# A one-core transformer block kernel whose layer changes are taken in token halves

## The chip, the core and the metric

The kernel runs on one core of one Trainium2 chip. The metric is the device time of one launch in microseconds, the median of the runs shown.

## What is computed

Five residual layers of 1024 channels over 512 tokens, all in float32: a gated delta-rule mixer, a short-convolution mixer, a mixer of block attention, pooling and spatial gating, a cross attention over 256 memory rows, and a gated feed-forward part. Around each mixer `f` stand two norms:

```python
h = rms_norm(x, pre_norm_w[i])
y = f(h)                          # products with w_in, the mixer, a product with w_out
x = x + rms_norm(y, post_norm_w[i])
```

`rms_norm` multiplies a token's row by one over the root of its mean square, then by a weight for each channel. It works on each token by itself, so one half of the tokens can be normed before the other.

## The kernel before, in words

Activations lie channel-major: a tile is 128 channels by 512 tokens, and `xT`, `h_hi`, `h_lo` and `y_T` hold eight tiles each (index `k`). Every large product is made of three (`product3`, L739): each operand is split into a rounded part `hi` and the remainder `lo`, and hi by hi, hi by lo and lo by hi are added in PSUM. One chunk is 128 output channels by 512 tokens: 8 tiles by 3 products, 24 matmuls, in one of the banks.

**Weights** come in slabs of 1024 by 256, two chunks each, in the order of `plan` (L286). SyncE loads a slab into one of two ring slots. ScalarE makes `w_hi` (`split_hi`, L1533) once the slab two before it has been used by TensorE; VectorE makes `w_lo` (`split_lo`, L2160). Seventeen slabs have their `w_lo` from GpSimd (L2899, L2906), among them `SC0`, `MIX0` and `FF1`, the first slabs of the layers 1, 2 and 4. TensorE waits for `split_ready` of a slab (`next_slab`, L705). All four queues run in the order written.

**A seam** is the passage from a layer's output product to the next layer's first chunks. The change touches three: the first (layer 0 to 1), the second (1 to 2) and the third (3 to 4). At each, before:

- TensorE makes the eight output chunks. In the first and second seam they stand in banks 0 to 7 (`out_tile` L831, `wide_out` L855), with 16 input tiles in two passes; in the third they rotate over four banks (`pair3`).
- ScalarE's `post_norm` (L1562) squares each chunk into `sq` and copies it into `y_T`. VectorE's `sum_squares` (L2191) adds the squares in `rs`. TensorE sums over the channels with a matmul by ones (`out_sum`, L770), in plain float32, and ScalarE's `inverse_rms` (L1550) makes the root's inverse by Ln and Exp.
- VectorE's `post_norm` (L2206) then takes tile by tile: multiply by `rs` (L2217), add to `xT` (L2221), and after ScalarE's `h_hi` (`pre_norm`, L1606) the remainder `h_lo` (L2225). A tree of seven additions (L2239) follows, for the next norm.
- TensorE's `first_four` (L784) first issues 14, 8 and 14 products that nobody reads (`keep_clock`, L779), in the seams one, two and three. Then it follows the tiles: for tile `k` four products with `h_hi` and two with `h_lo` for two chunks of the first slab, and half a tile's work (three products) of the second slab's two chunks. Nine such halves, 27 products, are left when the first slab is done, and `norm_sum` (L765) stands among them.
- The second slab is split by halves: ScalarE takes one half of its `w_hi` (`split_hi_half`, L1544), VectorE the other (`split_lo_halves`, L2168).

At the second seam, 32 transposes for a bias (L1228) and the ScalarE copies of them (L1905) also lie in this passage.

## Time and profile before

| What | us |
|---|---|
| Median of 3 runs (1804.18 to 1804.68) | 1804.19 |
| The profiled execution's own time | 1804.97 |
| Its span, first to last instruction | 1803.2 |
| TensorE busy in it (10559 matmuls) | 1777.8 |
| VectorE, ScalarE, GpSimd busy | 991.3, 722.9, 140.9 |

The profile shows one execution. Busy TensorE time contains overlapping matmuls, since a matmul's duration includes its way through the array; its rate is read from the distance between starts.

### The profile page before, as it was taken

The page shows a single profiled execution, that of the slowest core. Times are in us where ns is not written, and L with a number is a line of the kernel's source. Part 1 is how long each engine was busy: PE and PEld are TensorE (multiplying, and loading weights), DVE is VectorE, ACT ScalarE, POOL GpSimd, SP SyncE. Part 2 cuts the span into 40 slices and gives each one's busy share as a digit, 9 for nine tenths or more (in the row PEclk, how much of TensorE's full clock was granted, in tenths as well). Part 3 has the DMA queues.
Part 4 walks back from the last instruction along what each step waited for, and adds up shares of the span by engine and source line. Part 5 has one row for each costly group of instructions (what it writes and reads, how often), then busy time and mean ns, then how long its engine had stood idle before and what let it go on. Part 6 is the DMA issues. An engine that isn't in the chain of part 4 may idle for free.

```text
span 1803.2 us, 26545 instructions
## 1 busy us (share of the span) xinstructions
PE 1777.8 (99%) x10559; PEld 1437.7 (80%) x10559; DVE 991.3 (55%) x1666; ACT 722.9 (40%) x1382; POOL 140.9 (8%) x108
## 2 busy tenths in 40 slices
PE   8999999999999999999999999999999999999999
PEld 6788888887887888888888788468887778888887
DVE  4645656466636544454443746744424587777434
ACT  5645656547435212211124533754223532222324
POOL 1113031130002000000000101520000100000000
PEclk9999999999999999999999999999999999999999
DMA  6422212122235332222333451013313222223221
GB/s 194 84 54 76 63 49 78 55 71 62 83 109 124 110 100 93 93 93 93 101 106 98 91 117 48 24 48 117 117 47 117 70 93 93 93 94 110 98 77 65
DMA packets 183184, 158.18 MB, mean 88 GB/s; under 512 B 36978, under 2 KB 179887, under 8 KB 183051
## 3 DMA queue, kind: packets, MB, share of 16 engines
q1 hardware_dynamic: 172672, 152.88, 27.8%
q0 software_dynamic: 1248, 3.19, 1.2%
q10 hardware_dynamic: 9163, 0.72, 0.4%
q8 instruction: 70, 1.15, 0.3%
q14 instruction: 31, 0.25, 0.0%
HBM read 152.77 MB, written 3.73 MB: 87 GB/s over the span
## 4 chain that ended last, share of the span: by engine, by line
PE 90%; DVE 4%; ACT 3%; issue 1%; DMA 1%; ACTq 0%; SPq 0%; POOL 0%; DVEq 0%
PE bank L744 13%; PE bank L746 13%; PE bank L745 13%; PE bank L845 5%; PE bank L847 5%; PE bank L846 5%; PE bank L945 4%; PE bank L947 4%; PE bank L946 4%; PE bank L734 4%; PE bank L1072 1%; PE bank L1083 1%; PE bank L1139 1%; PE bank L1094 1%; PE bank L1338 1%
## 5 line engine op out<-in xcount | busy, mean ns | idle before, releaser
L1542 ACT ACTIVATE w_hi<-ring 128x2048 fp32r<-128x2048 f32 x122 | 234.0, 1918 | 535.6 <-PE bank L746 376.1
L744 PE MATMUL bank<-h_hi,w_hi 128*128 128x512 f32 x1024 | 400.4, 391 | 2.2 <-DVE w_lo L2165 2.0
L746 PE MATMUL bank<-h_hi,w_lo 128*128 128x512 f32 x1024 | 398.5, 389 | 0.0
L745 PE MATMUL bank<-h_lo,w_hi 128*128 128x512 f32 x1024 | 398.4, 389 | 0.0
L2165 DVE TENSOR_TENSOR w_lo<-ring,w_hi 128x2048 fp32r<-128x2048 f32 x105 | 240.4, 2290 | 247.9 <-ACT w_hi L1542 247.9
L744 PEld LDWEIGHTS bank<-h_hi,w_hi 128*128 128x128 f32 x1024 | 192.2, 188 | 44.9 <-issue 3.6
L745 PEld LDWEIGHTS bank<-h_lo,w_hi 128*128 128x128 f32 x1024 | 192.2, 188 | 40.2 <-issue 0.5
L746 PEld LDWEIGHTS bank<-h_hi,w_lo 128*128 128x128 f32 x1024 | 192.2, 188 | 40.1
L845 PE MATMUL bank<-h_hi,w_hi 128*128 128x512 f32 x432 | 170.5, 395 | 1.7 <-DVE arena L2854 1.0
L847 PE MATMUL bank<-h_hi,w_lo 128*128 128x512 f32 x432 | 168.3, 390 | 0.0
L846 PE MATMUL bank<-h_lo,w_hi 128*128 128x512 f32 x432 | 168.2, 389 | 0.0
L2903 POOL TENSOR_TENSOR w_lo<-ring,w_hi 128x2048 fp32r<-128x2048 f32 x16 | 73.5, 4591 | 1059.3 <-ACT w_hi L1542 1059.3
L945 PE MATMUL bank<-h_hi,w_hi 128*128 128x512 f32 x368 | 151.2, 411 | 0.0
L947 PE MATMUL bank<-h_hi,w_lo 128*128 128x512 f32 x368 | 143.9, 391 | 0.0
L946 PE MATMUL bank<-h_lo,w_hi 128*128 128x512 f32 x368 | 143.6, 390 | 0.0
L2260 DVE SCALAR_TENSOR_TENSOR arena<-arena,cols 128x511 f32<-128x511 f32 x120 | 90.1, 751 | 14.8 <-DVE arena L2260 0.3
L845 PEld LDWEIGHTS bank<-h_hi,w_hi 128*128 128x128 f32 x432 | 81.1, 188 | 18.6 <-issue 1.5
L847 PEld LDWEIGHTS bank<-h_hi,w_lo 128*128 128x128 f32 x432 | 81.1, 188 | 17.1
L846 PEld LDWEIGHTS bank<-h_lo,w_hi 128*128 128x128 f32 x432 | 81.2, 188 | 15.9
L947 PEld LDWEIGHTS bank<-h_hi,w_lo 128*128 128x128 f32 x368 | 69.1, 188 | 15.3
L945 PEld LDWEIGHTS bank<-h_hi,w_hi 128*128 128x128 f32 x368 | 69.2, 188 | 14.9 <-issue 1.9
L946 PEld LDWEIGHTS bank<-h_lo,w_hi 128*128 128x128 f32 x368 | 69.4, 188 | 11.8
(449 smaller groups left out, 2508.7 us busy)
## 6 DMA issues: line engine op xcount, KB each, us to landing
ring<-in_sc_w_in SPq DMA_DIRECT2D x32, 1024.0 KB, 5.4
ring<-in_gdn_w_in SPq DMA_DIRECT2D x24, 1024.0 KB, 5.4
ring<-in_w_up SPq DMA_DIRECT2D x22, 1024.0 KB, 5.1
ring<-in_gdn_w_out SPq DMA_DIRECT2D x8, 1024.0 KB, 5.2
ring<-in_sc_w_out SPq DMA_DIRECT2D x8, 1024.0 KB, 5.2
ring<-in_w_down SPq DMA_DIRECT2D x8, 1024.0 KB, 5.2
ring<-in_w_in SPq DMA_DIRECT2D x4, 1024.0 KB, 5.7
ring<-in_w_mk SPq DMA_DIRECT2D x4, 1024.0 KB, 5.2
```

Of the source, the lines that this page charges most:

```text
L744: pe.matmul(o, a_hi(k), b_hi(k), start=(k == tiles[0]), stop=False)
L745: pe.matmul(o, a_hi(k), b_lo(k), start=False, stop=False)
L746: mm = pe.matmul(o, a_lo(k), b_hi(k), start=False, stop=(k == tiles[-1]))
L845: pe.matmul(o, w_hi[:, st["slab"], w], h_hi[:, k, :], start=(a == 0 and k == 0), stop=False)
L846: pe.matmul(o, w_hi[:, st["slab"], w], h_lo[:, k, :], start=False, stop=False)
L847: mm = pe.matmul(o, w_lo[:, st["slab"], w], h_hi[:, k, :], start=False, stop=(a == last and k == kt - 1))
L945: pe.matmul(psum[b][:, :], w_hi[:, st["slot"], w], h_hi[:, k, :], start=(k == 0), stop=False)
L946: pe.matmul(psum[b][:, :], w_hi[:, st["slot"], w], h_lo[:, k, :], start=False, stop=False)
L947: mm = pe.matmul(psum[b][:, :], w_lo[:, st["slot"], w], h_hi[:, k, :], start=False, stop=(k == KD - 1))
L1542: act.activation(w_hi[:, plan[n]["pair"], :], ring[:, n % 2, :], ACT.Copy).then_inc(w_hi_ready, 1)
L2165: dve.tensor_tensor(w_lo[:, plan[n]["pair"], :], ring[:, n % 2, :], w_hi[:, plan[n]["pair"], :].bitcast(F32), ALU.subtract)\
L2260: ins = dve.scalar_tensor_tensor(out=dst[:, s:S], in0=src[:, 0:S - s], scalar=weight(taps - 1 - s), in1=dst[:, s:S], op0=ALU.mult, op1=ALU ...
```

## The change

The last two output chunks of the three layers share one bank for each half of the tokens: columns 0 to 255 are the even chunk and 256 to 511 the odd one. TensorE computes the whole first half of the tokens (`halves_done`, n = 0), then the second. Square, copy, sum and root of the first half are issued while the second is computed. The next layer's tiles 0 to 4 come as ten units of 256 tokens (five of the first half, five of the second), tiles 5 to 7 whole. TensorE follows these 13 units (`first_units`): the second slab's products for the units 0 to 3 are made together at unit 4, and from then on each unit has six products of either slab. `keep_clock` is no longer called at the seams. The half splits are gone: the second slab's `w_hi` is made whole by ScalarE between the units 2 and 3, its `w_lo` whole by VectorE before unit 5. The `w_lo` of `SC0`, `MIX0` and `FF1` goes from GpSimd to VectorE. `norm_sum` moves: into chunk 4 at the first seam, among the bias transposes at the second, to the end of `first_units` at the third. The bias transposes go behind `first_units`. At the first seam chunks 4 to 6 use banks 4 to 6.

```diff
+        HALVED, BY_HALF = (0, 1, 3), 5
+        units_of = lambda layer: [(k, half) for half in halves for k in range(BY_HALF)] + [(k, every) for k in range(BY_HALF, KD)] \
+            if layer in HALVED else [(k, every) for k in range(KD)]
...
-            def first_four(parts, idle):
...
-                keep_clock(4, idle)
...
+            def half_out(slab, bank, k, n, opens=False, closes=False):
+                for side in range(2):
+                    o, w = bank[:, halves[side]], slice(k * 256 + P * side, k * 256 + P * side + P)
+                    pe.matmul(o, w_hi[:, slab, w], h_hi[:, k, halves[n]], start=(opens and k == side == 0), stop=False)
+                    pe.matmul(o, w_hi[:, slab, w], h_lo[:, k, halves[n]], start=False, stop=False)
+                    mm = pe.matmul(o, w_lo[:, slab, w], h_hi[:, k, halves[n]], start=False, stop=(closes and k == KD - 1 and side == 1))
+                return mm
+            def halves_begun():
...
+                for k in range(KD):
+                    for n in range(2):
+                        mm = half_out(slab, psum[6 + n], k, n, opens=True)
...
+            def halves_done(slab, banks, totals, opens=False, within=lambda k: None):
...
+                for n in range(2):
+                    for k in range(KD):
...
+                        if k == KD - 3:
+                            pe.wait_ge(square_used, base + KD - 2)
+                            pe.matmul(totals[n][:, 0:S // 2], ones, rs[:, halves[n]], start=True, stop=False)
+                        if n and k == 0:
+                            half_sum(totals, 0)
+            def half_sum(totals, n):
+                pe.wait_ge(square_ready, 8 * st["layer"] + KD - 1 + n)
+                pe.matmul(totals[n][:, 0:S // 2], ones, sq[:, 0, halves[n]], start=False, stop=False)
+                pe.matmul(totals[n][:, 0:S // 2], ones, sq[:, 1, halves[n]], start=False, stop=True).then_inc(square_used, 1)
+            def first_units(totals):
...
+                for u, (k, i) in enumerate(units):
+                    pe.wait_ge(h_hi_ready, at + u + 1)
+                    high_products(slab, banks, k, i)
+                    if u == BY_HALF - 1:
+                        slab1 = next_slab()
+                        banks += [take_bank(None) for _ in range(2)]
+                        for earlier in units[:u]:
+                            second_products(slab1, banks, *earlier)
+                    pe.wait_ge(h_ready, at + u + 1)
+                    low_products(slab, banks, k, i)
+                    if u == BY_HALF - 2:
+                        half_sum(totals, 1)
+                        st["layer"] += 1
+                    if u >= BY_HALF - 1:
+                        second_products(slab1, banks, k, i)
```

ScalarE, `post_norm` and `pre_norm`:

```diff
+                    if early is not None and k == KD - 2:
...
+                        half_squares(st["open"][0][0], layer, 0)
+                        half_copies(st["open"][0][0], layer, 0)
+                        st["layer"] += 1
+                        half_rms(totals[0], layer, 0)
+                        return
...
+                for u, (k, i) in enumerate(units_of(layer - 1)):
+                    act.wait_ge(x_ready, units_before(layer - 1) + u + 1)
+                    act.activation(h_hi[:, k, i], xT[:, k, i], ACT.Copy, scale=PRE[layer](k)).then_inc(h_hi_ready, 1)
+                    if i.stop == S:
+                        act.activation(y_T[:, k, :], xT[:, k, :], ACT.Square).then_inc(x_squared, 1)
+                        between(k)
+                    elif u == BY_HALF - 3:
+                        banks, totals, second = st["open"]
+                        split_hi(second)
+                    elif u == BY_HALF - 2:
+                        half_squares(banks[1], layer - 1, 1)
+                    elif u == BY_HALF - 1:
+                        half_copies(banks[1], layer - 1, 1)
+                        half_rms(totals[1], layer - 1, 1)
```

VectorE, `post_norm`:

```diff
+                dve.wait_ge(rms_ready, roots_before(layer) + 1)
+                for u, (k, i) in enumerate(units):
+                    opens_half = i.start and k == 0
+                    if opens_half:
+                        split_lo(second)
+                        low_part(u - 1)
+                        dve.wait_ge(rms_ready, roots_before(layer) + 2)
+                    scaled(k, i)
+                    if u and not opens_half:
+                        low_part(u - 1)
+                    added(k, i)
```

GpSimd:

```diff
-            split_lo(SC0)
...
-            split_lo(MIX0)
...
-            split_lo(FF1)
```

## Rows read from the trace of the kernel before

**Rows 1.** The page: busy time (part 1), chain by engine (part 4).
```profile
PE 1777.8 (99%) x10559; PEld 1437.7 (80%) x10559; DVE 991.3 (55%) x1666; ACT 722.9 (40%) x1382; POOL 140.9 (8%) x108
...
PE 90%; DVE 4%; ACT 3%; issue 1%; DMA 1%; ACTq 0%; SPq 0%; POOL 0%; DVEq 0%
```

**Rows 2.** Timeline of PE (start, duration, us): full-width products, three issues apart.
```profile
557.71 0.39 PE L845 MATMUL bank<-h_hi,w_hi 128*128 128x512 f32 x1
...
558.39 0.39 PE L845 MATMUL bank<-h_hi,w_hi 128*128 128x512 f32 x1
```

**Rows 3.** Timeline of PE: products over 256 columns, 33 issues apart.
```profile
1034.86 0.28 PE L744 MATMUL bank<-w_hi,h_hi 128*128 128x256 f32 x1
...
1038.82 0.28 PE L744 MATMUL bank<-w_hi,h_hi 128*128 128x256 f32 x1
```

**Rows 4.** Timeline, first seam: from the last product to the next layer's.
```profile
559.75 1.02 PE L774 MATMUL bank<-rs,masks 128*128 128x512 f32 x2
559.95 0.60 ACT L1560 ACTIVATE sq<-bank 128x512 f32<-128x512 f32 x1 [3.31 <-PE bank L847]
...
560.61 1.12 PE L776 MATMUL bank<-sq,masks 128*128 128x512 f32 x2
...
561.77 0.69 ACT L1552 ACTIVATE rs<-bank,small 128x512 f32<-128x512 f32 x1 [0.64 <-PE bank L776]
...
563.16 0.69 DVE L2217 TENSOR_TENSOR arena<-arena,rs 128x512 f32<-128x512 f32 x1 [0.68 <-ACT rs L1554]
...
564.61 0.72 ACT L1610 ACTIVATE h_hi<-xT,cols 128x512 fp32r<-128x512 f32 x1 [1.49 <-DVE xT L2221]
...
565.37 0.75 DVE L2225 SCALAR_TENSOR_TENSOR h_lo<-xT,cols,h_hi 128x512 fp32r<-128x512 f32 x1 [0.19 <-ACT h_hi L1610]
...
565.48 0.47 PE L820 MATMUL bank<-h_hi,w_hi 128*128 128x512 f32 x1 [0.56 <-ACT h_hi L1610]
```

**Rows 5.** Timeline at the first seam: the end of the first four chunks.
```profile
581.08 4.54 DVE L2239 TENSOR_TENSOR arena<-arena 128x512 f32<-128x512 f32 x7
...
582.83 1.92 ACT L1542 ACTIVATE w_hi<-ring 128x2048 fp32r<-128x2048 f32 x1 [1.94 <-PE bank L827]
...
585.54 2.28 DVE L2165 TENSOR_TENSOR w_lo<-ring,w_hi 128x2048 fp32r<-128x2048 f32 x1
...
585.97 1.02 PE L768 MATMUL bank<-arena,masks 128*128 128x512 f32 x2
...
587.06 0.39 PE L811 MATMUL bank<-h_lo,w_hi 128*128 128x512 f32 x1
...
589.98 0.47 PE L744 MATMUL bank<-h_hi,w_hi 128*128 128x512 f32 x1 [0.23 <-DVE arena L2540]
```

**Rows 6.** Timeline of PE, second seam: sum, transposes, first row chunk.
```profile
1003.51 1.02 PE L774 MATMUL bank<-rs,masks 128*128 128x512 f32 x2
...
1005.42 1.22 PE L1231 MATMUL bank<-masks,arena 31*128 31x31 f32 x32
...
1034.06 0.36 PE L744 MATMUL bank<-w_hi,h_hi 128*128 128x256 f32 x1
```

**Rows 7.** Timeline of PE, third seam: sum, fifth chunk's first product.
```profile
1420.94 1.02 PE L774 MATMUL bank<-rs,masks 128*128 128x512 f32 x2
...
1450.79 0.39 PE L744 MATMUL bank<-h_hi,w_hi 128*128 128x512 f32 x1
```

**Rows 8.** Groups by line and shape (busy us, mean ns): 256 columns.
```profile
L1984 ACT ACTIVATE arena<-bank,small 128x256 f32<-128x256 f32 x4 | 1.9, 471 | 9.5 <-PE bank L746 9.5
L2292 DVE TENSOR_TENSOR ws<-arena,ws 128x256 fp32r<-128x256 f32 x1 | 0.4, 421 | 0.0
```

**Rows 9.** The page, part 5: the slab remainders that POOL computes.
```profile
L2903 POOL TENSOR_TENSOR w_lo<-ring,w_hi 128x2048 fp32r<-128x2048 f32 x16 | 73.5, 4591 | 1059.3 <-ACT w_hi L1542 1059.3
```

**Rows 10.** First products, and their stretch (PE, PEld, DVE, ACT, POOL, PEclk, DMA, GB/s).
```profile
17.74 0.47 PE L890 MATMUL bank<-h_hi,w_hi 128*128 128x512 f32 x1 [2.66 <-DVE h_lo L2288]
...
16.00:24.00 8.00, 6.26 (x20) 4.84 (x21) 6.67 (x9) 6.89 (x11) 4.57 (x1) 0.79 0.64 169
```

More of the change, by code:

```diff
@@ L494, in build @@
         square_sum = y_T[:, 0, :]
+        HALVED, BY_HALF = (0, 1, 3), 5
+        halves, every = [slice(0, S // 2), slice(S // 2, S)], slice(0, S)
+        roots_before = lambda layer: 2 * layer + sum(n < layer for n in HALVED)
+        units_of = lambda layer: [(k, half) for half in halves for k in range(BY_HALF)] + [(k, every) for k in range(BY_HALF, KD)] \
+            if layer in HALVED else [(k, every) for k in range(KD)]
+        units_before = lambda layer: sum(len(units_of(n)) for n in range(layer))
         rs_squared = sq[:, 0, :]
@@ L800, in first_four @@
-                    low_products(slab, first, k)
-                for n in range(KD - 1, 2 * KD):
-                    half_tile(slab1, later, n)
-                    if n == KD + 3:
-                        norm_sum()
-            def half_tile(slab, banks, n):
-                k, side = n // 2, n % 2
-                b, w = banks[side], slice(k * 256 + P * side, k * 256 + P * side + P)
-                pe.matmul(psum[b][:, :], w_hi[:, slab, w], h_hi[:, k, :], start=(k == 0), stop=False)
-                pe.matmul(psum[b][:, :], w_hi[:, slab, w], h_lo[:, k, :], start=False, stop=False)
-                mm = pe.matmul(psum[b][:, :], w_lo[:, slab, w], h_hi[:, k, :], start=False, stop=(k == KD - 1))
-                if k == KD - 1:
-                    mm.then_inc(chunk_done, 1)
@@ new lines, in second_products @@
+            def second_products(slab, banks, k, i):
+                for side in range(2):
+                    o, w = psum[banks[2 + side]][:, i], slice(k * 256 + P * side, k * 256 + P * side + P)
+                    pe.matmul(o, w_hi[:, slab, w], h_hi[:, k, i], start=(k == 0 and i.start == 0), stop=False)
+                    pe.matmul(o, w_hi[:, slab, w], h_lo[:, k, i], start=False, stop=False)
+                    mm = pe.matmul(o, w_lo[:, slab, w], h_hi[:, k, i], start=False, stop=(k == KD - 1))
+                    if k == KD - 1:
+                        mm.then_inc(chunk_done, 1)
@@ L819, in high_products @@
+            def high_products(slab, banks, k, i):
+                for side, b in enumerate(banks[0:2]):
                     w = slice(k * 256 + P * side, k * 256 + P * side + P)
-                    pe.matmul(psum[b][:, :], w_hi[:, slab, w], h_hi[:, k, :], start=(k == 0), stop=False)
-                    pe.matmul(psum[b][:, :], w_lo[:, slab, w], h_hi[:, k, :], start=False, stop=False)
-            def low_products(slab, banks, k):
-                for side, b in enumerate(banks):
+                    pe.matmul(psum[b][:, i], w_hi[:, slab, w], h_hi[:, k, i], start=(k == 0 and i.start == 0), stop=False)
+                    pe.matmul(psum[b][:, i], w_lo[:, slab, w], h_hi[:, k, i], start=False, stop=False)
@@ L826, in low_products @@
+            def low_products(slab, banks, k, i):
+                for side, b in enumerate(banks[0:2]):
                     w = slice(k * 256 + P * side, k * 256 + P * side + P)
-                    mm = pe.matmul(psum[b][:, :], w_hi[:, slab, w], h_lo[:, k, :], start=False, stop=(k == KD - 1))
+                    mm = pe.matmul(psum[b][:, i], w_hi[:, slab, w], h_lo[:, k, i], start=False, stop=(k == KD - 1))
                     if k == KD - 1:
@@ L1569, in post_norm @@
                         split_hi(early)
-                    if k == KD - 1 and early is not None:
-                        split_hi_half(early + 1)
+                    if early is not None and k == KD - 2:
+                        first, totals = st["chunk"], (psum[4:6] if wide else [psum[7], psum[6]])
+                        st["open"] = [psum[6 + n if wide else (first + n) % 4][:, :] for n in range(2)], totals, early + 1
+                        half_squares(st["open"][0][0], layer, 0)
[3 more added lines that the diff above has]
+                        return
                     act.wait_ge(chunk_done, n + 1)
@@ L2208, in post_norm @@
                 layer = st["layer"]
[L2209 removed]
+                sum_squares(ahead, beside, KD - 1 if second is None else KD - 2)
                 if second is not None:
[L2211 to L2212 removed]
+                    split_lo(second - 1)
                 if layer == 0:
                     dve.wait_ge(x_back, KD)
[L2216 to L2217 removed]
@@ new lines, in post_norm @@
+                dve.wait_ge(rms_ready, roots_before(layer) + 1)
[9 more added lines that the diff above has]
+                    added(k, i)
+                    if i == every and k:
+                        between(k)
```

186 lines of the change are left out of this document (94 added, 92 removed).

## The prediction

> **What bounds the kernel.** The page comes first: TensorE is busy for 1777.8 us of a span of 1803.2, and 90% of the chain that ended last lies on it [rows 1]. A change can gain only where TensorE waits or issues work that nobody reads, and it loses with every nanosecond that a needed product takes longer. The waits of TensorE name the seams, so the timelines of the three seams are what decides. At the first, the last product's successor starts at 559.75 and the next layer's first product at 565.48: 5.7 us, filled by the sum of squares, fourteen idle products and a wait [rows 4]. I count a seam from the end of its last output product to the start of the fifth chunk (the first row chunk at the second seam): 589.98 - 559.75 = 30.2 us, 1034.06 - 1003.51 = 30.6, 1450.79 - 1420.94 = 29.9 [rows 4 to 7]. Needed in each are 96 products and the norm's sum. Three products take 0.68 us, so one takes 0.2267 [rows 2], and 96 take 21.8. The norm's sum takes 587.06 - 585.97 less a product, 0.86 [rows 5]. What is left, **7.6, 7.9 and 7.2 us**, is all that the change can work on. That is 22.7 us in all.
>
> **What the halves cost.** Thirty-three issues of a product over 256 columns take 3.96 us, 0.120 each [rows 3]. Two halves take 0.240 against 0.2267 for one whole: 13.3 ns more for each product that is split. The first and second seam split 48 in the first pass of the output product, 48 in its last slab, and 5 tiles x 4 chunks x 3 = 60 in the next layer: 156, 2.1 us. The third has no first pass: 108, 1.4 us. In all 420, 5.6 us. The rows have other operands in the two roles, but TensorE's work for them is the same in kind, and I take their value. The ends are no loss at all (width alone) and twice it. The Trainium skill, "TensorE: Matmul & The Clock Gate", section "Back-to-back issue gap", gives an issue's gap as its columns at 2.4 GHz and 2.5 ns more; by it 420 splits would cost 1.1 us, and my sum would come out 4.5 us lower. The rows speak against it here.
>
> The sums of squares go from two float32 matmuls of full width to six of half width. At 0.43 us for a half (0.86 halved) that is 2.6 us a seam, all of it between needed products; before, its 1.7 us lay in the 5.7. If a half took as long as a whole, it would be 2.6 us more a seam; width counts in rows 2 and 3, so I stay near the half.
>
> **The chain of the first half.** Let 0 be the end of the first half's products. ScalarE starts its squares 0.20 after it and the sum can start at 0.86, as in rows 4. TensorE is then 0.72 us (six halves) into the second half: a wait of 0.1. The Ln comes at 2.02 (561.77 - 559.75). From it to the multiplication take 1.39 us and on to `h_hi` 1.45 [rows 4]. At half width ScalarE saves about 0.21 an operation (0.69 to 0.47) and VectorE 0.27 (0.69 to 0.42) [rows 4, 8], so `h_hi` starts at 2.02 + 0.97 + 0.91 = 3.9. Then a unit takes a round of `h_hi` 0.51, remainder 0.48, addition 0.42: 1.4 us. The third `h_hi` ends at 3.9 + 2.8 + 0.5 = 7.2. TensorE's second half takes 48 x 0.12 + 0.1 + 0.86 + 0.43 = 7.2 too. So units 0 to 2 are ready just in time and the old hole of 5.7 us is gone. This is the gain.
>
> **The wait in the middle.** ScalarE's `split_hi` of the second slab stands behind unit 2 in its queue and waits for the end of the second half (its pair of `w_hi` is in use till then): 7.4 to 9.3, since a slab takes 1.92 [rows 5]. Behind it wait `h_hi` of unit 3 (to 9.8) and the second half's squares (to 10.3). VectorE's remainder of unit 3 and the addition of unit 4 end at 10.6, then its `split_lo` of 2.28 [rows 5] ends at 12.9. TensorE has from 7.2 on 24 + 4 halves and the second sum, 3.4 + 0.86 = 4.2 us, and needs that slab next. It waits 12.9 - 7.2 - 4.2 = 1.5 us, in one or two pieces. Ends: 0 and 3. The second half's own chain is no wait: `rs` is ready about 12.9, unit 5 at 14.6, while TensorE has 24 + 2 + 6 halves (3.8 us) up to 16.8. From there a unit is 12 halves, 1.44 us, against VectorE's 1.4, and a whole tile 2.7 against some 2.15. TensorE is the bound again and VectorE gets ahead. Its tree of 4.54 us [rows 5] is done in time.
>
> **The wait at the end.** This is what speaks against the change. The third slab's `w_hi` may be written when the first slab is done. Before, 27 products and the norm's sum (7.0 us) were left at that point. Now six are left, 1.36 us, since the second slab keeps step. The third slab needs ScalarE 0.26 after it, then 1.92, VectorE 2.28, and about 0.1 for signals: 4.55 us [rows 5]. TensorE **waits 3.2 us** at the first seam. At the other two the next chunk needs also a bank that VectorE empties only behind that `split_lo` (0.69 us, as rows 4 have it): 5.25 - 1.36 - 0.86 (the norm's sum, which runs meanwhile) = 3.0. At the second seam the 32 bias transposes (1.1 us in the issues of rows 6, where they lay in the old hole) and the turning of `rs` fit into these 3.0, and cost nothing more. The bank wait that before stood ahead of the fifth chunk goes by the new banks 4 to 6, and is in the 7.6.
>
> **The rest.** GpSimd's three `w_lo` of 4.59 us [rows 9] become VectorE's of 2.28: VectorE has nothing else between the sixth square and the root, so nothing waits. SyncE's load of the fourth slab waits for the second slab's split and comes some 5 us later; it is needed 15 us after. At the second seam SyncE's small loads and a conv slab are behind it and move by some 4 us; they cost nothing while the slab that follows is not issued before the third slab is split. ScalarE copies the bias after the norm's root, ahead of the row chunks, and has caught up before its third eviction.
>
> **The sum.** New, other than the 96 products and the norm's sum: first seam 2.1 + 2.6 + 0.1 + 1.5 + 3.2 = 9.5 against 7.6, so +1.9; second 2.1 + 2.6 + 0.1 + 1.5 + 3.0 = 9.3 against 7.9, +1.4; third 1.4 + 2.6 + 0.1 + 1.5 + 3.0 = 8.6 against 7.2, +1.4. Together **+4.7 us**. The profiled execution took 1804.97, 0.8 above the median of 1804.19, and would take 1809.7; the median goes to **1808.9**.
>
> **The rivals.**
> - *The halves are cheap*: a split product costs nothing beyond its columns. Then 5.6 us fall away: 1803.3. Rows 3 speak against it. 0.10.
> - *No wait in the middle*: ScalarE and VectorE get the second slab done within TensorE's 4.2 us. 4.5 us less: 1804.4. 0.18.
> - *The end is covered* (faster): the third slab is split in time, and the waits of 3.2, 3.0 and 3.0 us are not there: 1799.7. It decides at 4.55 us of TensorE work behind the first slab's last product; I count 1.36. 0.06.
> - *The clock falls*: in this trace TensorE waited 2.66 us ahead of 17.74, after small transposes, and in 16 to 24 us the granted clock was 0.79 of 2.4 GHz: 42% of 8 us at 1.2 GHz, which loses 1.7 us [rows 10]. The new waits of 3 us could do the same, now that the idle products are gone: 3 x 1.7 = 5.1, 1814.0. Against it: dense products stand ahead of each. 0.14.
> - *It doesn't do what it says*: the first half's chain is longer than the second half's products (7.2 us), and the old hole comes back in part. A unit that takes 0.35 us longer makes 1.0 a seam: 1811.9. 0.10.
>
> My forecast has the remaining 0.42; its own range is 1806.5 to 1811.5. The range reaches to the rivals on both sides but the fastest: 1803.2 to 1814.2. A difference under 0.2%, 3.6 us, can't be told from none. Slower by more (above 1807.8): 0.36 of the forecast and the last two rivals, 0.60. Same: the rest of it and the first two, 0.34. Faster: 0.06.
>
> **What would show it.** Right: no wait of TensorE at a seam's first unit; a wait for `w_lo` of the second slab of about 1 us; three waits near 3 us behind the first four chunks, released by VectorE; TensorE's issues over 256 columns at 0.12; granted clock at 2.4 GHz throughout. Wrong: the third slab's split ready before TensorE asks, a seam of under 29 us by the same count, or a clock that falls after the waits.

## The result, and the profile of the changed kernel

The changed kernel took 1812.28 us in the median of five runs (1811.08 to 1813.93), the kernel before, in the same rounds, 1804.18 (1801.99 to 1804.68): a ratio of 1.0046, 95% interval 1.0034 to 1.0057. That is 0.46% slower, 8.1 us. It lies in the range on record (1803.2 to 1814.2) and on the side that the chances favoured, but outside the likeliest case's own range, which ended at 1811.5. The profiled execution took 1813.93 with a span of 1812.1, 8.9 us more than before.

The page, busy time and chain, against [rows 1]:

```profile
PE 1782.8 (98%) x10967; PEld 1463.7 (81%) x10967; DVE 991.6 (55%) x1705; ACT 729.4 (40%) x1409; POOL 126.6 (7%) x105
...
PE 89%; DVE 4%; ACT 3%; issue 2%; DMA 1%; ACTq 0%; SPq 0%; POOL 0%; DVEq 0%
```

TensorE is busy 5.0 us longer, although the 36 idle products (8.2 us at 0.2267 each) are gone from its work, and the span is 8.9 us longer, so 3.9 us more of it are waiting. The list of TensorE's waits names the new ones (us in total, times, longest):

```profile
PE bank L750 <- DVE w_lo L2253: 4.0, 3, 3.1
PE bank L750 <- DVE arena L2939: 2.8, 1, 2.8
...
PE bank L859 <- DVE w_lo L2253: 2.1, 3, 0.7
```

L750 is the first product of an ordinary chunk, L859 the first of the second slab. The six waits for `h_hi` that the kernel before had at its seams (3.0 us) are gone; three of 0.3 us, one a seam, have come in their place. The timeline of PE at the first seam puts them in order (start, duration; in brackets the wait and its releaser):

```profile
562.26 0.28 PE L796 MATMUL bank<-h_hi,w_lo 128*128 128x256 f32 x1
562.38 0.28 PE L869 MATMUL bank<-h_hi,w_hi 128*128 128x256 f32 x1
...
587.15 0.39 PE L861 MATMUL bank<-h_hi,w_lo 128*128 128x512 f32 x1
590.64 0.50 PE L750 MATMUL bank<-h_hi,w_hi 128*128 128x512 f32 x1 [3.10 <-DVE w_lo L2253]
590.98 0.40 PE L751 MATMUL bank<-h_lo,w_hi 128*128 128x512 f32 x1
591.22 0.57 PE L752 MATMUL bank<-h_hi,w_lo 128*128 128x512 f32 x1
591.58 1.91 PE L774 MATMUL bank<-arena,masks 128*128 128x512 f32 x2
592.50 1.42 PE L750 MATMUL bank<-h_hi,w_hi 128*128 128x512 f32 x1
593.72 0.63 PE L751 MATMUL bank<-h_lo,w_hi 128*128 128x512 f32 x1
594.14 0.63 PE L752 MATMUL bank<-h_hi,w_lo 128*128 128x512 f32 x1
594.57 0.45 PE L750 MATMUL bank<-h_hi,w_hi 128*128 128x512 f32 x1
```

The last product of the second half (L796) is followed by the next layer's first one 0.12 us later: the old hole of 5.7 us is closed, as foretold. In its place stands a wait of 3.10 us, and behind that something which the hole did not have: the norm's sum takes 1.91 us instead of 1.02, and the products start 0.42 apart (593.72, 594.14) instead of 0.23. The stretches show why (columns as in [rows 10]; the granted clock is the third number from the end):

```profile
588.00:592.00 4.00, 1.36 (x4) 1.09 (x5) 2.29 (x1) 0.19 (x1) 0.00 (x0) 0.91 0.01 5
592.00:596.00 4.00, 4.00 (x11) 2.52 (x10) 1.06 (x2) 2.44 (x3) 0.00 (x0) 0.66 0.82 256
1052.00:1056.00 4.00, 3.22 (x26) 3.01 (x25) 2.89 (x3) 1.00 (x1) 0.00 (x0) 0.94 0.00 0
1056.00:1060.00 4.00, 4.00 (x13) 3.18 (x12) 3.86 (x5) 0.00 (x0) 0.00 (x0) 0.64 0.97 212
1456.00:1460.00 4.00, 1.24 (x3) 1.05 (x4) 3.93 (x4) 2.56 (x3) 0.00 (x0) 0.78 0.09 24
1460.00:1464.00 4.00, 4.00 (x15) 3.19 (x15) 3.86 (x7) 0.98 (x2) 0.00 (x0) 0.79 0.69 238
```

TensorE drops to its lower level, 1.2 GHz, once in or behind each seam: in or behind the end wait of the first and of the third, and at the second behind the hidden sums, 17 us after the seam (`hidden_sums`, 16 float32 products over 64 columns in the next layer's attention, two records each). Behind those sums there is a wait of 0.78 us:

```profile
1050.96 3.72 PE L1276 MATMUL bank<-arena,ring 128*128 128x64 f32 x32
1055.45 0.80 PE L750 MATMUL bank<-h_hi,w_hi 128*128 128x512 f32 x1 [0.78 <-DVE w_lo L2253]
1056.04 0.63 PE L751 MATMUL bank<-h_lo,w_hi 128*128 128x512 f32 x1
```

The kernel before has the same sums, 3.72 us long, and the same wait of 0.78 us behind them, and goes on at 0.23 us a product. So that wait is not new, only what the clock does after it.

**Where the 8.9 us are.** I take the time of one product in both traces and subtract: the difference is how much later the changed kernel is at that point. For each seam there is a point ahead (the first seam: the product at 490.73 in the trace of before; the third: the product pass at 1373.83) and one behind (611.83, 1070.71 and 1495.82; the first seam's end is the second's beginning). What is left over is not of the seams: the layers ahead, where nothing was changed, came out 0.54 us shorter (in the other traces -2.18 to +0.35), the stage between the second and the third seam 0.08 shorter, the end 0.5 longer. In the table are the same differences for all kernels of this study, each in its one profiled execution, and beside them the measured ratio. Three traces (high products first, second slab's products late, and the one with 3 idle products) are 1.5 us longer between the second and the third seam as well, by a fall of the clock at 1120 us, in a stage that nobody edited; that is not in their sums.

| kernel | first seam | second | third | sum, us | ratio to before (95%) |
|---|---|---|---|---|---|
| forecast | +1.9 | +1.4 | +1.4 | +4.7 | |
| the change | +3.78 | +3.25 | +2.01 | +9.04 | 1.0046 (1.0034 to 1.0057) |
| idle products in its waits | +2.19 | +1.62 | +2.00 | +5.81 | 1.0035 (1.0022 to 1.0047) |
| before, without idle products | +1.62 | +2.10 | -0.02 | +3.70 | 1.0021 (1.0011 to 1.0031) |
| high products first | +2.91 | +0.74 | +1.11 | +4.76 | 1.0029 (1.0019 to 1.0040) |
| second slab's products late | -0.71 | +1.99 | +1.82 | +3.10 | 1.0029 (1.0017 to 1.0042) |
| the two, and GpSimd's additions | +2.14 | +3.83 | +2.02 | +7.99 | 1.0046 (1.0030 to 1.0062) |
| the same with 3 idle products | +2.18 | +3.80 | +2.01 | +7.99 | 1.0049 (1.0033 to 1.0065) |
| four tiles by halves | +2.69 | +2.15 | +3.66 | +8.50 | 1.0057 (1.0038 to 1.0076) |
| mended | -0.75 | +0.74 | +1.13 | +1.12 | 1.0012 (1.0003 to 1.0021) |
| before, VectorE splits | +0.04 | 0.00 | +0.02 | +0.06 | 1.0006 (0.9997 to 1.0015) |

### The profile page after: what moved, and what is told of

Read it like the earlier page. It is cut to its first block, busy times and chain, and to the rows that moved or that the text cites. A ratio compares the mean times of both kernels' runs of the same rounds, so it can differ in the third digit from the quotient of the medians.

```text
span 1812.1 us, 27418 instructions
## 1 busy us (share of the span) xinstructions
PE 1782.8 (98%) x10967; PEld 1463.7 (81%) x10967; DVE 991.6 (55%) x1705; ACT 729.4 (40%) x1409; POOL 126.6 (7%) x105
## 4 chain that ended last, share of the span: by engine, by line
PE 89%; DVE 4%; ACT 3%; issue 2%; DMA 1%; ACTq 0%; SPq 0%; POOL 0%; DVEq 0%
PE bank L750 13%; PE bank L752 13%; PE bank L751 13%; PE bank L894 5%; PE bank L895 5%; PE bank L896 5%; PE bank L997 4%; PE bank L740 4%; PE bank L999 4%; PE bank L998 4%; PE bank L796 1%; PE bank L795 1%; PE bank L794 1%; PE bank L1124 1%; DVE w_lo L2253 1%
## 5 line engine op out<-in xcount | busy, mean ns | idle before, releaser
L1605 ACT ACTIVATE w_hi<-ring 128x2048 fp32r<-128x2048 f32 x125 | 239.6, 1917 | 541.6 <-PE bank L752 375.5
L750 PE MATMUL bank<-h_hi,w_hi 128*128 128x512 f32 x1008 | 396.9, 394 | 6.9 <-DVE w_lo L2253 4.0
L2253 DVE TENSOR_TENSOR w_lo<-ring,w_hi 128x2048 fp32r<-128x2048 f32 x111 | 254.1, 2289 | 259.9 <-ACT w_hi L1605 259.9
L752 PE MATMUL bank<-h_hi,w_lo 128*128 128x512 f32 x1008 | 393.8, 391 | 0.0
L751 PE MATMUL bank<-h_lo,w_hi 128*128 128x512 f32 x1008 | 393.7, 391 | 0.0
L750 PEld LDWEIGHTS bank<-h_hi,w_hi 128*128 128x128 f32 x1008 | 190.3, 189 | 50.6 <-DVE w_lo L2253 4.5
L751 PEld LDWEIGHTS bank<-h_lo,w_hi 128*128 128x128 f32 x1008 | 190.3, 189 | 40.2 <-issue 1.0
L752 PEld LDWEIGHTS bank<-h_hi,w_lo 128*128 128x128 f32 x1008 | 190.1, 189 | 39.8
L997 PE MATMUL bank<-h_hi,w_hi 128*128 128x512 f32 x368 | 151.2, 411 | 0.0
L894 PE MATMUL bank<-h_hi,w_hi 128*128 128x512 f32 x368 | 145.5, 395 | 1.7 <-DVE arena L2939 1.0
L999 PE MATMUL bank<-h_hi,w_lo 128*128 128x512 f32 x368 | 143.9, 391 | 0.0
L998 PE MATMUL bank<-h_lo,w_hi 128*128 128x512 f32 x368 | 143.6, 390 | 0.0
L896 PE MATMUL bank<-h_hi,w_lo 128*128 128x512 f32 x368 | 143.3, 390 | 0.0
L895 PE MATMUL bank<-h_lo,w_hi 128*128 128x512 f32 x368 | 143.3, 390 | 0.0
L894 PEld LDWEIGHTS bank<-h_hi,w_hi 128*128 128x128 f32 x368 | 69.1, 188 | 16.2 <-issue 1.4
L999 PEld LDWEIGHTS bank<-h_hi,w_lo 128*128 128x128 f32 x368 | 69.1, 188 | 15.3
L2988 POOL TENSOR_TENSOR w_lo<-ring,w_hi 128x2048 fp32r<-128x2048 f32 x13 | 59.5, 4579 | 312.3 <-ACT w_hi L1605 312.3
L997 PEld LDWEIGHTS bank<-h_hi,w_hi 128*128 128x128 f32 x368 | 69.2, 188 | 14.9 <-issue 1.9
L896 PEld LDWEIGHTS bank<-h_hi,w_lo 128*128 128x128 f32 x368 | 69.1, 188 | 14.6
L895 PEld LDWEIGHTS bank<-h_lo,w_hi 128*128 128x128 f32 x368 | 69.2, 188 | 13.3
L998 PEld LDWEIGHTS bank<-h_lo,w_hi 128*128 128x128 f32 x368 | 69.4, 188 | 11.8
```

Of the source, the lines that this page charges most:

```text
L750: pe.matmul(o, a_hi(k), b_hi(k), start=(k == tiles[0]), stop=False)
L751: pe.matmul(o, a_hi(k), b_lo(k), start=False, stop=False)
L752: mm = pe.matmul(o, a_lo(k), b_hi(k), start=False, stop=(k == tiles[-1]))
L894: pe.matmul(o, w_hi[:, st["slab"], w], h_hi[:, k, :], start=(a == 0 and k == 0), stop=False)
L895: pe.matmul(o, w_hi[:, st["slab"], w], h_lo[:, k, :], start=False, stop=False)
L896: mm = pe.matmul(o, w_lo[:, st["slab"], w], h_hi[:, k, :], start=False, stop=(a == last and k == kt - 1))
```

## The experiments

**Does the clock cost it? Idle products in the new waits.** The edit, in the changed kernel:

```
             first_units(psum[4:6])
+            keep_clock(7, 13)
             for n in range(4, 8):
...
             hidden_sums(0)
+            keep_clock(7, 3)
             pair3()
...
             norm_sum()
+            keep_clock(6, 12)
```

> The changed kernel with idle products in its three gaps: 13 behind the first four chunks at the first seam (a wait of 3.10 us), 12 behind the norm's sum at the third (2.84 us), 3 ahead of the pair that follows the hidden sums at the second (0.78 us). Nothing else changes, and each lot is as long as the wait that it fills (0.2267 us each). Theory: the change cost 8.1 us instead of 4.7 because the granted clock falls in and after these gaps, 1.5 to 1.6 us each time. With the gaps filled it stays at 2.4 GHz: the waits stay as long as they are, and the time falls by 3 x 1.6 = 4.8 us, to about 1807.5. Rival: the clock falls for another reason (the run as a whole has less clock, or the fall at 1056 us of the second seam comes from the sparse work at 1035 to 1039 us, well ahead of it): then the second seam keeps its fall (3.2 us gained, 1809.1), or nothing is gained (1812.3), or the idle products themselves push the next product late (slower than 1812.3).

Measured: 1811.29 us, ratio 1.0035. The granted clock stays at 2.4 GHz at all three places:

```profile
587.86 3.11 PE L788 MATMUL bank<-exact 128*128 128x512 f32 x13
591.13 0.50 PE L750 MATMUL bank<-h_hi,w_hi 128*128 128x512 f32 x1 [0.16 <-DVE w_lo L2256]
591.47 0.39 PE L751 MATMUL bank<-h_lo,w_hi 128*128 128x512 f32 x1
```

```profile
592.00:596.00 4.00, 4.00 (x17) 2.94 (x16) 1.59 (x3) 2.98 (x3) 0.00 (x0) 1.00 0.83 249
```

The same stretch had 0.66 in the changed kernel. The first two seams are shorter by 1.59 and 1.63 us, the price that was expected. The third is not shorter at all (+2.01 and +2.00), though its clock is back too. The reason stands 13 us behind it: the kernel before waits there 1.24 us for a later slab's `w_lo`, and this run does so for 1.51, the changed kernel for 0.16. First this run, then the changed kernel:

```profile
1468.72 0.49 PE L750 MATMUL bank<-h_hi,w_hi 128*128 128x512 f32 x1 [1.51 <-DVE w_lo L2256]
```

```profile
1471.45 0.49 PE L750 MATMUL bank<-h_hi,w_hi 128*128 128x512 f32 x1 [0.16 <-DVE w_lo L2253]
```

What the slow products lost, this wait gave back. So in these two traces the clock cost the change 3.2 us, not 4.8, and without it the change costs 5.8. The measured ratios differ by 0.0011, 2.0 us, and their intervals overlap, so by the times alone the two kernels are not told apart. The mean granted clock of each execution does tell them apart: 0.996 or 0.997 in all five of the changed kernel, 0.998 or 0.999 in all six of this run.

**Who sets the third seam.** It is VectorE. Its queue in the kernel before, then in the changed kernel: `w_lo` of the third slab, the first chunk taken out of its bank, `w_lo` of the later slab.

```profile
1446.72 2.29 DVE L2165 TENSOR_TENSOR w_lo<-ring,w_hi 128x2048 fp32r<-128x2048 f32 x1
1449.61 0.69 DVE L2854 TENSOR_TENSOR arena<-bank,rs 128x512 f32<-128x512 f32 x1 [0.61 <-ACT rs L1554]
...
1460.65 2.29 DVE L2165 TENSOR_TENSOR w_lo<-ring,w_hi 128x2048 fp32r<-128x2048 f32 x1
```

```profile
1455.82 2.29 DVE L2253 TENSOR_TENSOR w_lo<-ring,w_hi 128x2048 fp32r<-128x2048 f32 x1 [1.54 <-ACT w_hi L1605]
1458.02 0.68 DVE L2939 TENSOR_TENSOR arena<-bank,rs 128x512 f32<-128x512 f32 x1
...
1469.04 2.29 DVE L2253 TENSOR_TENSOR w_lo<-ring,w_hi 128x2048 fp32r<-128x2048 f32 x1
```

From the first row with `rs` to the last row VectorE never waits, 11.0 us in both. So the seam costs what that first row is late. Counted from the product ahead of the seam (1373.83 before, 6.41 later in this trace), it is 2.00 us late in the changed kernel and in the run with idle products. In the kernels below it is late by 1.13 (high first), 1.80 (late), 2.01 and 1.98 (GpSimd), 1.13 (mended), and each time the third seam costs the same within 0.03; only with four tiles by halves it is 2.58 against 3.66, since a fall stands beside it. The start of the chain is the predicted one: the third slab's `w_hi` waits for the first slab's last product, and VectorE waits for `w_hi`.

**Does a hole cost the kernel before as much?** Its own idle products taken out (`keep_clock(4, idle)` in `first_four`, 36 products in all).

> The kernel before without the 14, 8 and 14 idle products of its three seams; its holes of 5.7 us are as long as they were, but TensorE has only the norm's two sums (and the bias transposes at the second) to do in them. Theory of the clock: a hole of some 3.5 to 4 us without work costs what it costs in the changed kernel, about 1.6 us in each of the three seams, 1809.0. Rival: the clock fell in the changed kernel for some other reason than idle time; then this kernel takes the 1804.2 of before, and its granted clock stays at 2.4 GHz in the seams.

Measured: 1808.62 us, ratio 1.0021, so 3.8 us slower than with them. The timeline of PE at the first seam, and its stretches:

```profile
560.51 1.12 PE L776 MATMUL bank<-sq,masks 128*128 128x512 f32 x2
565.37 0.77 PE L819 MATMUL bank<-h_hi,w_hi 128*128 128x512 f32 x1 [3.74 <-ACT h_hi L1609]
565.93 0.63 PE L820 MATMUL bank<-h_hi,w_lo 128*128 128x512 f32 x1
```

```profile
564.00:568.00 4.00, 2.63 (x6) 2.15 (x7) 3.63 (x6) 2.48 (x4) 4.00 (x8) 0.59 1.07 297
568.00:572.00 4.00, 4.00 (x12) 3.08 (x11) 3.62 (x7) 2.31 (x4) 1.21 (x3) 0.56 1.08 200
1012.00:1016.00 4.00, 3.86 (x11) 2.67 (x10) 3.62 (x6) 3.38 (x6) 0.00 (x0) 0.59 1.09 286
1052.00:1056.00 4.00, 3.44 (x9) 2.67 (x10) 3.90 (x6) 0.00 (x0) 0.00 (x0) 0.60 0.61 146
```

The clock falls at the first seam, at the second, and again behind the hidden sums. At the third seam TensorE waits 3.7 us as well and the clock does not fall (no stretch of 4 us from 1420 to 1480 is under 0.98, and the difference is -0.02 us). Taking the idle products out brought falls, and idle time does not always bring one. Behind the hidden sums the same work and the same wait stood before a fall in the changed kernel and in this one, and before none in the kernel before and in the next two runs below; those two had a fall at 1120 us instead, in a stage that nobody edited. The price of a fall that nothing absorbs is steady, 1.5 to 1.6 us; whether it comes is not. (The fall at 1012 us is mostly absorbed: the row chunk behind it is 0.53 us late, and the rest of this seam's 2.10 is the fall behind the hidden sums.)

All nine executions of this kernel have a mean granted clock of 0.993 to 0.995, the 20 of the kernel before beside them 0.998 to 1.000. Those 20 vary by the clock too: the medians are 1803.3, 1805.0 and 1806.3 us at 1.000, 0.999 and 0.998.

**The wait in the middle.** At unit 4, the fifth half tile, the high products of the second slab come first, since they need only ScalarE's part of the split:

```
-                        slab1 = next_slab()
...
+                        pe.wait_ge(w_hi_ready, nxt["splits"])
                         banks += [take_bank(None) for _ in range(2)]
                         for earlier in units[:u]:
-                            second_products(slab1, banks, *earlier)
+                            second_high(slab1, banks, *earlier)
+                        assert next_slab() == slab1
+                        for earlier in units[:u]:
+                            second_low(slab1, banks, *earlier)
```

> The changed kernel, but behind the fourth tile's half TensorE takes the 16 products of the second slab's high part first (they need only ScalarE's split) and the 8 of the low part after VectorE's. The wait for w_lo of the second slab, 0.70 us at each seam, should go: 3 x 0.7 = 2.1 us, to about 1810.2. If the wait in the middle were no loss, because VectorE's tiles of the second half hold TensorE up anyway (a unit takes VectorE 1.40 us, TensorE 1.44), the same 0.7 us would come back as a wait for h_lo or h_hi of the following units, and the time would stay at 1812.3. With the first slab's end 0.7 us earlier the third slab's split is earlier too, so the end waits should stay as long as they are.

Measured: 1810.97 us, ratio 1.0029. The wait of 0.70 us for the second slab's `w_lo` is off the list at all three seams, and the first and third seam are 0.87 and 0.90 us shorter; the second is 2.51 shorter, of which 1.6 is the fall behind the hidden sums, which this trace doesn't have. The gain is 0.87 and not 0.70 because the wait is longer than its entry: by the distance of starts (567.20 due, 568.06 in the changed kernel) it is 0.86. The rival, VectorE's tiles as the bound, is out: TensorE was the bound in the middle. The falls at the first and third seam are still there, and the one at 1120 us has come, so the whole trace is only 2.2 us shorter than the changed kernel's.

**The end wait.** The second slab's products of the last half unit and of the three whole tiles (6 over a half and 18 whole, 4.8 us) stand behind the first slab's last product; at the first seam VectorE splits the third slab inside its tree of additions, and the norm's sum comes three tiles later.

```
-                    if u >= BY_HALF - 1:
+                    if BY_HALF - 1 <= u < 9:
                         second_products(slab1, banks, k, i)
+                for u in range(9, len(units)):
+                    second_products(slab1, banks, *units[u])
...
+                    if far == 1 and third is not None:
+                        split_lo(third)
```

> The changed kernel with the second slab's products of the last half unit and of the three whole tiles (48 issues' worth of 24 product pairs, 4.8 us of TensorE work) moved behind the first slab's last product, at all three seams; at the first seam VectorE also splits the third slab inside its tree of squares, and the norm's sum comes three tiles later in the fifth chunk. Theory: the end wait is there because only 1.36 us of work are left when the first slab's pair comes free, and 4.55 are needed. First seam: the wait of 3.10 us goes and with it the clock's fall of 1.6: 4.4 us less. Third: the bank waits for VectorE behind the tree and the norm's sum, which do not move, so the wait only shrinks by what the third slab's split no longer adds (0 to 1 us). Second: 0 to 0.5 us. Together about 1807.5. Rival: the first slab's products then catch up with VectorE's tiles (1.40 us for a half, 2.15 for a whole one), TensorE waits for h_lo instead, and the end wait only changes its place: 1812.3.

(The "48 issues' worth of 24 product pairs" of the expectation is a miscount of these 24 products; the 4.8 us are right, by the starts below.) Measured: 1810.27 us, ratio 1.0029. At the first seam the wait is gone and no fall follows; PE, then ACT and DVE of the same stretch:

```profile
582.74 0.62 PE L878 MATMUL bank<-h_lo,w_hi 128*128 128x512 f32 x2
583.21 0.28 PE L861 MATMUL bank<-h_hi,w_hi 128*128 128x256 f32 x1
...
587.80 0.39 PE L863 MATMUL bank<-h_hi,w_lo 128*128 128x512 f32 x1
588.03 0.40 PE L750 MATMUL bank<-h_hi,w_hi 128*128 128x512 f32 x1
```

```profile
583.47 1.92 ACT L1607 ACTIVATE w_hi<-ring 128x2048 fp32r<-128x2048 f32 x1 [1.28 <-PE bank L878]
```

```profile
585.49 2.29 DVE L2255 TENSOR_TENSOR w_lo<-ring,w_hi 128x2048 fp32r<-128x2048 f32 x1 [0.64 <-ACT w_hi L1607]
```

The first slab ends at 583.21, the third is split at 587.78, TensorE comes for it at 588.03: 4.57 us needed, 4.82 there. That is the point of 4.55 us that the prediction gave. The seam went from +3.78 to -0.71, 4.5 us, as expected. At the other two the bank waits for the tree, the norm's sum and the root, none of which moved: the third still waits 2.16 us. The second gained nothing: its +1.99 is without a fall, and the changed kernel with idle products has +1.62.

**Shortening the tree: GpSimd.** The high products first and the postponed products at all seams, without the split inside the tree; GpSimd takes three of the tree's seven additions, and the norm's sum comes ahead of the last 12 postponed products:

```
+            def pairs_of(layer):
+                for k in range(0, KD - 2, 2):
+                    pool.wait_ge(x_squared, 8 * layer + k + 2)
+                    pool.tensor_tensor(y_T[:, k, :], y_T[:, k, :], y_T[:, k + 1, :], ALU.add).then_inc(pairs_summed, 1)
```

> The changed kernel with four alterations: the second slab's high products first (as in the run before), its products of the last half unit and the three whole tiles behind the first slab's last product (as in the run before), the first three of the seven additions of the square tree given to GpSimd, which has nothing to do then (pairs 0+1, 2+3, 4+5, each as soon as ScalarE has squared it), and the norm's sum issued inside the postponed products. Theory: behind the last h_lo VectorE needs 4 additions (2.6 us), then TensorE 0.9, ScalarE 1.4, VectorE 0.7: 5.8 us to a free bank, and TensorE has 0.4 + 4.8 + 0.9 = 6.1 us of work. The end waits go at all three seams, and with them the falls of the clock. Against the kernel before: first seam about -1.4 us, second about 0 (its transposes are real work) unless the clock falls behind the hidden sums (+1.6), third about -1.0. Together 2 us faster than before, 1803. Rival: GpSimd's additions are slower than the tiles come, or slow VectorE down beside them, so that the tiles, now the bound, come later: waits for h_hi and h_lo in the tiles, no faster than the 1810 of the postponed products alone.

Measured: 1813.67 us, ratio 1.0046. No end wait is left at any seam and the clock falls at none, and yet nothing is won. The rival came, and the timelines of GpSimd and of VectorE show it in the first addition:

```profile
571.86 1.31 POOL L3037 TENSOR_TENSOR arena<-arena 128x512 f32<-128x512 f32 x1 [118.24 <-ACT arena L1711]
```

```profile
571.93 1.52 DVE L2311 TENSOR_TENSOR arena<-arena,rs 128x256 f32<-128x256 f32 x1
```

VectorE's multiplication, 0.42 us elsewhere, takes 1.52 while GpSimd adds; a whole tile's multiplication at 575.51 and its addition at 579.75 take 1.78 instead of 0.68. Three holds of 1.1 us lengthen the chain of tiles, and TensorE waits for `h_hi` four times, 3.2 us at each seam.

The same kernel with three idle products behind the hidden sums:

> The run above with 3 idle products in the wait of 0.78 us behind the first hidden sums of the second seam, where the granted clock fell in the changed kernel and in the bare one, and not in the kernel before. Theory of the clock: no fall there; the same time as the run above if that one shows no fall either, 1.6 us less if it does. Rival: the clock falls all the same, later in the stage, and the idle products change nothing.

Measured: 1814.48 us, ratio 1.0049: the same as the run above within the intervals. Neither trace has a fall behind the hidden sums, so the idle products were not put to the test there. But this trace has one at 1120 us (0.67 and 0.90 in 1120 to 1128), 1.5 us, which the run above has not: the rival's fall "later in the stage" came.

**Four tiles by halves** (`BY_HALF = 4` in place of 5).

> The changed kernel with four tiles by halves instead of five. My account of the middle: 12 fewer split products a seam at 13.3 ns (0.5 us in all three); the second slab's split stands one unit earlier in both queues, so w_lo comes 1.4 us earlier, while TensorE has one unit and six halves less ahead of it (0.7 us): the wait of 0.7 us for it goes, and the second half's tiles still come in time behind 24 halves of the second slab. The end waits stay. About 0.9 us less a seam, 1809.6. Rival: with one half tile less TensorE reaches the second half's first unit too early and waits for h_hi there, 0.5 to 1.5 us a seam: 1812 or more.

Measured: 1814.97 us, ratio 1.0057, and the wait of 0.70 us is still there. My account was wrong in its reason: ScalarE's split of the second slab starts at 562.50, when the second half's last product lets go of the old `w_hi`, whatever stands ahead of it in the queue. One unit earlier in the queue only puts it ahead of the third tile's `h_hi`, which TensorE needs sooner; its wait for `h_hi` grows from 0.30 to 1.03 us. Its end wait at the first seam is 3.10 us, as in the changed kernel, and no fall follows; so its first two seams, +2.69 and +2.15, compare with the +2.19 and +1.62 of the run with idle products, 0.5 us more each. The third has a fall as long as the one at the first seam of the kernel without idle products (0.56 and 0.59 in 1456 to 1464). The order with five tiles was the better one.

**VectorE in GpSimd's place, alone.** The kernel before with only that part of the change:

```
-            split_lo(SC0)
...
                 if second is not None:
+                    split_lo(second - 1)
                     split_lo_halves(second)
```

> The kernel before with only the last part of the change: the three first slabs that GpSimd split (4.6 us each) are split by VectorE behind its sum of squares (2.28 us each). My prediction put nothing on this. The run with GpSimd's additions showed VectorE held up while GpSimd works (0.42 us became 1.52, 0.68 became 1.78), and in the kernel before an addition of VectorE at the first seam took 4.33 us beside GpSimd's split. Theory: that addition comes back to 0.69, the sum's seventh addition is 3.6 us earlier, but TensorE doesn't use it, since its last products end at 559.7 and the root waits for them: 0 us, within 0.5. Rival: the hold was on the chain (the addition ended at 559.48, TensorE's sum began at 559.75), and its end makes the first seam shorter by up to 0.5 us, or VectorE's half splits now stand behind the whole one and the first slab's first product waits: slower by 1 to 2 us a seam.

Measured: 1805.15 us, ratio 1.0006, and no difference in any seam. In the kernel before VectorE's seventh addition of the sum of squares, beside GpSimd's split from 554.31 to 558.93, took 4.33 us; here it takes 0.69. First before, then this run:

```profile
555.15 4.33 DVE L2203 TENSOR_TENSOR rs<-rs,sq 128x512 f32<-128x512 f32 x1 [6.16 <-ACT sq L1560]
```

```profile
552.95 0.69 DVE L2203 TENSOR_TENSOR rs<-rs,sq 128x512 f32<-128x512 f32 x1 [6.16 <-ACT sq L1560]
```

The 3.6 us were off the path: the sum in TensorE stands behind the last output product anyway. The prediction's zero holds.

**The change, mended.** High products first at all seams; postponed products and the split inside the tree at the first; one addition of the tree in VectorE's idle time ahead of the last `h_lo`; the norm's sum ahead of the bias transposes; idle products in what waits are left.

```
+                dve.wait_ge(x_squared, 8 * layer + 2)
+                own.did(dve.tensor_tensor(y_T[:, 0, :], y_T[:, 0, :], y_T[:, 1, :], ALU.add))
                 low_part(len(units) - 1)
```

> The changed kernel with what the runs so far bear out, and without GpSimd: the second slab's high products first at all three seams; the postponed products and the third slab's split inside the tree at the first seam alone; one of the seven additions of the tree (0+1) in VectorE's idle time ahead of the last h_lo (0.79 us); the norm's sum ahead of the bias transposes at the second seam; 3 idle products ahead of the second seam's pair and 9 in the third seam's end wait. From the traces: first seam -1 us against the kernel before (-0.71 in the run with postponed products), second 0.7 less 0.65 and 0.3, about 0, third 1.1 less 0.65, about +0.5, each without a fall of the clock. Together the time of the kernel before, 1805, within 1.5 us; 7 to 8 us faster than the changed kernel. Rival: the gains overlap (VectorE's tiles are the bound and high products first gain nothing there), 1807 to 1808.

Measured: 1806.17 us, ratio 1.0012: some 6 us better than the change, and 2.2 us (0.5 to 3.8) behind the kernel before. It lies within the first case, 1805 and 1.5 us more, near its edge. But the seams are not the expected ones: -0.75, +0.74 and +1.13 against -1, 0 and +0.5. The first gained nothing beyond the run with postponed products (-0.71): there the tiles are the bound by now (three waits for `h_hi`, 1.0 us). The second and third are those of the run with high products first (+0.74 and +1.11), so the addition and the norm's sum that were moved gained nothing: VectorE is done with the tree early and waits 1.27 us for the third slab's `w_hi`.

```profile
1448.82 2.29 DVE L2275 TENSOR_TENSOR w_lo<-ring,w_hi 128x2048 fp32r<-128x2048 f32 x1 [1.27 <-ACT w_hi L1627]
```

The combination that could release it sooner, products postponed at these two seams as well, with the earlier norm's sum and without GpSimd, was not run. No version that beats both kernels by what can be measured came out of this.

## Why the prediction was right in direction and short by 3.4 us

The work and the waits that it names are there: 5.8 us of the trace's 9.0, against 4.7 forecast. The other 3.2 us are the clock, which it had as a rival.

- **The hole goes: right.** 0 is at 555.11; the first `h_hi` starts at 559.07, 3.96 later (3.9 forecast), and the first unit follows the last half product at once.
- **Split products, 13.3 ns each: right.** Halves start 0.12 apart throughout. The 48 of the first pass moved the first seam's transposes from 0.54 us ahead of the kernel before to 0.12 behind, 0.66 (0.64 forecast). The rule of the Trainium skill, "TensorE: Matmul & The Clock Gate", section "Back-to-back issue gap", would have made the sum 4.5 us lower; this trace doesn't agree with it for these products. The rival of cheap halves is out.
- **Sums of squares, 2.6 us a seam: near.** At the first seam the pair of L829 and L830 holds TensorE from 555.96 to 556.74, and the next product takes 0.18 longer; with the 0.43 of L822 that is 1.39 for the first half. The second has 0.86 (565.87 to 566.54 and 0.19 more) and 0.43: 2.7 for both.
- **The wait in the middle, 1.5 us: near, and in two pieces as foretold.** By the distance of starts it is 0.46 + 0.86 = 1.3 (the entries 0.30 and 0.70 count from the end of the last product, which reaches past the time when the next could have started). The second slab's `w_lo` ends at 568.00, 12.89 after 0, forecast 12.9. The run with high products first, 0.87 and 0.90 us shorter at two seams, shows that the second piece was on the path.
- **The end waits, 3.2, 3.0, 3.0 us: right.** From the second slab's last product to the fifth chunk 590.64 - 587.38 = 3.26; at the others 3.96 and 3.86, less the 0.86 of the norm's sum: 3.1 and 3.0. At the second the bias transposes fill most of it (waits of 0.34 and 0.27 are left), as foretold. The kernel with postponed products shows the cause and the deciding point.
- **The work of a seam without the clock: 5.8 us against 4.7.** Seam by seam 2.19, 1.62 and 2.00 against 1.9, 1.4 and 1.4. By the prediction's own count, up to the fifth chunk, the third is 1.6 us late; what it costs is set behind that point, by VectorE's queue, which the prediction didn't follow so far (2.00). The terms as measured at the first seam, 2.1 + 2.7 + 0.1 + 1.3 + 3.3 = 9.5, make its +1.9 again; the 0.3 that are left there and the 0.2 at the second I did not assign.
- **The step that failed: "granted clock at 2.4 GHz throughout".** The prediction had the mechanism as a rival at 0.14, three falls at 1.7 us, and set dense products ahead of each wait against it. That was no protection: at the first seam 25 us without a longer wait than 0.7 us stood ahead of the 3.10 us. The falls came, at 1.5 to 1.6 us each, and cost 3.2 us in all in the trace, since at the third seam a wait that was there before took it up. It is partly luck that they came in it at all three places: four tiles by halves had the same 3.10 us and no fall there. But the mean clock of 0.996 or 0.997 in all five executions, against 0.998 or 0.999 with idle products, says that this kernel has falls each time. Where they came I had wrong as well: the second was not at the seam but 17 us behind it. The kernel before carried 36 idle products for just this, worth 3.8 us by the run without them; the change took them out and put new waits in, and I counted only what room they took up.
- **A test that I worded badly.** A seam "of under 29 us by the same count" was to speak against the forecast. The first seam is 590.64 - 562.38 = 28.3 us by that count, only because the norm's sum (0.86) now stands behind the count's end.

## What to carry to other kernels

Before taking out work whose results nobody reads, ask what the granted clock does in the gap without it, and price a new TensorE wait of some 3 us at its length and allow for 1.6 us more, unless a wait behind it takes that up: of the ten waits of 2.2 to 3.7 us at the seams of these traces, eight had a fall in or behind them. When two slabs of weights are worked in step, neither comes free until the end: postponing one slab's products by as long as the third's preparation takes (4.6 us here) closed the gap at the seam where nothing else held the bank. Follow the other engines' queues beyond the seam: where one of them runs without a wait up to something that TensorE waits for, its start sets the cost, and filling TensorE's waits gains nothing. An idle GpSimd was no free helper beside a VectorE on the critical chain: each of its additions held VectorE up by 1.1 us.

## What the runs showed that was not expected

- While GpSimd runs an elementwise operation on two SBUF tiles, an operation of VectorE that begins beside it ends only 0.3 to 0.6 us after GpSimd's does: 0.42 us became 1.52, 0.68 became 1.78 (beside 1.3 to 1.4 us), 0.69 became 4.33 (beside 4.62). The Trainium skill, "SBUF — State Buffer", section "SBUF: two separate sides", has the rule: the two engines share a port pair by an exclusive lock, and whichever begins second waits for the whole instruction of the other, also where VectorE's operation has two SBUF inputs. The durations here agree with it. By it the rival of the GpSimd run was the case to expect.
- A fall of TensorE's clock is not tied to a wait alone: the same 3.72 us of sums and 0.78 us of wait stood ahead of a fall in two kernels and of none in six others; a bare wait of 3.7 us at one seam brought a fall while one of the same length at another did not, and the wait of 3.10 us had one behind it in two traces and none in a third.
- The kernel before varies with the clock too, from one execution to the next: 1.3 to 1.7 us for each 0.001 of mean granted clock in 20 executions.
